# Per-layer gate of a decoder trunk: seven half-size products for each pair of full tiles, the 64-token tile last

## What is computed

```python
    h = h + moe
    u = rmsnorm(h, norm_ple)
    gate = jax.nn.sigmoid(jnp.einsum('bld,de->ble', u, w_ple_gate))   # 1024 x 1024
    h = h + gate * jnp.einsum('blp,pd->bld', p_l, w_ple_proj)         # 256 x 1024
    return h, ...
# then y = rmsnorm(h, norm_final)
```

## Time and profile before

| | us |
|---|---|
| median of 3 runs | 834.19 |
| lowest, highest | 830.54, 836.55 |
| the profiled execution | 832.21 |
| its span | 830.4 |

### The profile page before, as it was taken

The page is one execution under the profiler, slowest core; times in us unless marked ns, Lnnn a source line. Parts: engine busy times, 40 slices in busy tenths (PEclk is TensorE's granted clock), DMA queues, the critical chain, the costliest instruction groups (busy, mean ns, idle before and its releaser), DMA issues. The chain is left out here.

```text
span 830.4 us, 12851 instructions
## 1 busy us (share of the span) xinstructions
PE 810.4 (98%) x5194; PEld 509.7 (61%) x5194; DVE 385.0 (46%) x859; ACT 214.2 (26%) x463; POOL 151.0 (18%) x182
## 2 busy tenths in 40 slices
PE   9999999999999999999999999999999999998996
PEld 4545777887889987777777776456343333344452
DVE  3223457584666523664853558636341111106443
ACT  3211152339324311121101101122121111124554
POOL 0234321004055224200220043000100001004000
PEclk9999999999999999999999999999999999999999
DMA  9520354403020200522252024036899999987111
GB/s 359 206 101 9 124 181 152 134 39 109 2 103 3 84 20 13 202 80 94 101 203 87 16 101 176 9 127 252 307 367 399 425 420 415 410 313 221 57 39 51
DMA packets 20896, 135.23 MB, mean 163 GB/s; under 512 B 2420, under 2 KB 3060, under 8 KB 13668
## 3 DMA queue, kind: packets, MB, share of 16 engines
q1 hardware_dynamic: 13392, 103.34, 31.9%
q0 software_dynamic: 4720, 23.83, 8.0%
q10 hardware_dynamic: 2724, 7.21, 2.7%
HBM read 118.94 MB, written 19.63 MB: 167 GB/s over the span
## 5 line engine op out<-in xcount | busy, mean ns | idle before, releaser
L791 PE MATMUL pair<-mem 128*128 128x288 f32 x640 | 158.9, 408 | 0.0
L791 PEld LDWEIGHTS pair<-mem 128*128 128x128 f32 x640 | 120.5, 190 | 35.4 <-ACT mem L1435 2.1
L961 PE MATMUL single<-mem 128*128 128x288 f32 x448 | 110.1, 407 | 0.2
L961 PEld LDWEIGHTS single<-mem 128*128 128x128 f32 x448 | 84.8, 190 | 25.6 <-issue 1.6
L1346 PE MATMUL single<-mem 128*32 128x512 f32 x768 | 85.1, 594 | 0.9 <-DVE mem L2382 0.9
L1435 ACT ACTIVATE mem<-single 128x256 f32<-128x256 f32 (+5 forms) x109 | 44.6, 419 | 126.8 <-PE single L1209 48.5
L1435 ACT ACTIVATE mem<-pair 128x512 f32<-128x512 f32 (+5 forms) x78 | 33.5, 480 | 165.2 <-PE pair L791 63.1
L1414 PE MATMUL pair<-mem 128*128 128x512 f32 (+1 forms) x192 | 63.3, 524 | 0.0
L1346 PEld LDWEIGHTS single<-mem 128*32 128x32 f32 x768 | 23.7, 110 | 52.7 <-issue 51.6
L2375 DVE SCALAR_TENSOR_TENSOR mem<-single,mem 128x256 f32<-128x256 f32 x12 | 5.8, 484 | 102.3 <-PE single L1346 91.1
L1200 PE MATMUL pair<-mem 128*128 128x512 f32 x112 | 51.0, 601 | 0.0
(11 more groups left out here) (412 smaller groups left out, 1095.1 us busy)
## 6 DMA issues: line engine op xcount, KB each, us to landing
mem<-in_w_gu SPq DMA_DIRECT2D x17, 2048.0 KB, 14.4
mem<-in_w_down SPq DMA_DIRECT2D x17, 1024.0 KB, 14.0
y_slots<-mem SPq DMA_DIRECT2D x9, 512.0 KB, 11.2
y_slots<-in_zeros POOLq DMA_DIRECT2D x8, 512.0 KB, 8.5
mem<-in_w_ga SPq DMA_DIRECT2D x2, 2048.0 KB, 7.6
mem<-in_w_gb SPq DMA_DIRECT2D x2, 2048.0 KB, 7.8
mem<-in_w_wo SPq DMA_DIRECT2D x2, 2048.0 KB, 7.7
mem<-in_w_pg SPq DMA_DIRECT2D x2, 2048.0 KB, 18.2
```

The lines of the kernel that those rows point to most:

```text
L791: last = nc.tensor.matmul(pb[:, hf, 0:HALF], w(k), rhs[:, k, hf * HALF:(hf + 1) * HALF], start=(k == 0), stop=(k == kk - 1))
L961: last = nc.tensor.matmul(single[plan.buf[s]][:, 0:HALF], lhs[:, k, :], rhs[:, k, :], start=(k == 0 and j in (0, 1, 3, 4)), stop=(k == 3), ...
```

## The change

For a pair of full tiles (0 and 1, then 2 and 3) the gate product is taken as one product of a 2 x 2 block matrix (tile by half of the 1024 input channels) by a 2 x 2 block matrix (half of the input channels by half of the output channels). It is computed by seven half-size products (Winograd's form of Strassen's scheme) in place of eight. Each is 4 steps of 128x128 by 128x512. For that:

- DVE forms four sums of weights once (`pg_t1` to `pg_t4`, 128x2048 each, the third in two parts of 1024) and four sums of rows for each pair (128x512 each, one in place).
- Two of the seven accumulate onto a bank that already holds another product, and one more does after that. ACT copies the banks' states that are needed apart to `sgp` (`keep`, four for each pair), and DVE adds the bank to the kept part (`out`, four for each pair). The sigmoid then reads SBUF, not PSUM.
- The order of tiles is `LAST = [0, 1, 2, 3, 4]`: the 64-token tile is last, with its products as before.
- The squares and roots of the rows (`row_root`) are spread among the gates.
- `p_product(4)` stands ahead of `u3_transpose(0)`; tile 0's last combination is split in two halves, and its first four chunks are transposed after the first; the first product waits for the first four chunks alone.
- In the last expert phase the second of the two PSUM banks is copied by DVE rather than ACT, and the small transpose of the overflow block (`ov_hT`) moves from behind the last down product to its middle.
- The final stores are of 64 rows (tile 4) where they were of 128.

The core of the diff:

```diff
-LAST = [0, 1, 4, 2, 3]
+LAST = [0, 1, 2, 3, 4]
+PG_ORDER = ["p1", "p2", "p5", "u2", "p3", "p4", "p7"]
+KEPT = {(name, q): 6 + 4 * q + i for q in range(2) for i, name in enumerate(["p1", "p5", "u2", "p4"])}
...
+        pg_bank = [(pair[1][:, 0, :], pair[1][:, 1, :], pair[0][:, 0, :]), (pair[0][:, 1, :], pair[1][:, 1, :], pair[0][:, 0, :])]
...
@@ PE, last down product
+                    if p == NPH - 1 and n == 0:
+                        ov_hT(0)
...
             down(NPH - 1)
-            ov_hT(0)
             ov_down(0)
...
@@ PE, the stage
+            p_product(NT - 1)
             u3_transpose(0)
-            p_product(NT - 1)
...
+            def gate_part(bank, rows, weights, start):
+
+                for c in range(4):
+                    last = nc.tensor.matmul(bank, rows(c), weights(c), start=(start and c == 0), stop=(c == 3), skip_group_check=True)
+                return last
+
+            for q in range(2):
+                bank_a, bank_b, bank_c = pg_bank[q]
+                first, second = (lambda c: u3T[:, c, 2 * q * P:2 * q * P + P]), (lambda c: u3T[:, c, 2 * q * P + P:2 * q * P + 2 * P])
+                pe.wait_ge(sem("u3T"), 4 * q + 1)
+                pe.wait_ge(sem("w_pg"), 32)
+                pe.wait_ge(sem("pp"), 4 + q)
+                gate_part(bank_a, first, lambda c: w_pg[0][:, c, :], True).then_inc(sem("pg_mm"), 1)
+                u3_transpose(2 * q + 1)
+                pe.wait_ge(sem("u3T"), 4 * q + 2)
+                if q:
+                    pe.wait_ge(sem("pp"), KEPT["p4", 0])
+                gate_part(bank_b, lambda c: first(c + 4), lambda c: w_pg[0][:, c + 4, :], True).then_inc(sem("pg_mm"), 1)
+                pe.wait_ge(sem("pp"), 5)
+                pe.wait_ge(sem("pg_sum"), SUM_AT["s1", q])
+                gate_part(bank_c, lambda c: pg_s1[q][:, c, :], lambda c: pg_t1[:, c, :], True).then_inc(sem("pg_mm"), 1)
+                pe.wait_ge(sem("pp"), KEPT["p1", q])
+                pe.wait_ge(sem("pg_sum"), SUM_AT["s2", q])
+                gate_part(bank_a, lambda c: pg_s2[q][:, c, :], lambda c: pg_t2[:, c, :], False).then_inc(sem("pg_mm"), 1)
+                u3_transpose(2 * q + 2)
+                pe.wait_ge(sem("pp"), KEPT["p5", q])
+                pe.wait_ge(sem("pg_sum"), SUM_AT["s4", q])
+                gate_part(bank_c, lambda c: pg_s4[q][:, c, :], lambda c: w_pg[1][:, c + 4, :], False).then_inc(sem("pg_mm"), 1)
+                pe.wait_ge(sem("pg_sum"), max(SUM_AT["t4", 0], SUM_AT["c11", q]))
+                gate_part(bank_b, lambda c: second(c + 4), lambda c: pg_t4[:, c, :], True).then_inc(sem("pg_mm"), 1)
+                pe.wait_ge(sem("pp"), KEPT["u2", q])
+                pe.wait_ge(sem("pg_sum"), max(SUM_AT["t3", 0], SUM_AT["s3", q]))
+                gate_part(bank_a, second, lambda c: pg_t3[c // 2][:, c % 2, :], False).then_inc(sem("pg_mm"), 1)
...
@@ ACT: the helpers
-                copy(yb[b][:, 512:D], pair[b][:, 1, :]).then_inc(sem("y_ready"), 1)
+                if e_done < NPH:
+                    copy(yb[b][:, 512:D], pair[b][:, 1, :]).then_inc(sem("y_ready"), 1)
...
+            def keep(name, q):
+
+                act.wait_ge(sem("pg_mm"), 7 * q + PG_ORDER.index(name) + 1)
+                k, hf, bank = {"p1": (0, 0, 0), "u2": (0, 1, 0), "p4": (1, 0, 1), "p5": (1, 1, 2)}[name]
+                if q:
+                    act.wait_ge(sem("h4"), 2 * k + hf + 1)
+                copy(sgp[k][:, 512 * hf:512 * hf + 512], pg_bank[q][bank]).then_inc(sem("pp"), 1)
...
@@ DVE: the helpers
+            dve.wait_ge(sem("dn_mm"), NPH)
+            dve.wait_ge(sem("y_stored1"), 16 * ((NPH - 1) // 2))
+            V.tensor_copy(yb[1][:, 512:D], pair[1][:, 1, :]).then_inc(sem("y_ready"), 1)
...
+            def rows_1_2(q):
+
+                dve.wait_ge(sem("u3T"), 4 * q + 4)
+                V.tensor_tensor(pg_s1[q], rows(q, 1, 0), rows(q, 1, 1), ALU.add).then_inc(sem("pg_sum"), 1)
+                dve.wait_ge(sem("pg_sum"), SUM_AT["s1", q])
+                V.tensor_tensor(pg_s2[q], pg_s1[q], rows(q, 0, 0), ALU.subtract).then_inc(sem("pg_sum"), 1)
...
+            def out(name, q):
+
+                after, k, hf, kept, bank = {"c11": ("p2", 0, 0, "p1", 1), "c12": ("p3", 0, 1, "u2", 2),
+                                            "c21": ("p7", 1, 0, "p4", 0), "c22": ("p7", 1, 1, "p5", 0)}[name]
+                h = sgp[k][:, 512 * hf:512 * hf + 512]
+                dve.wait_ge(sem("pg_mm"), 7 * q + PG_ORDER.index(after) + 1)
+                dve.wait_ge(sem("pp"), KEPT[kept, q])
+                V.tensor_tensor(h, pg_bank[q][bank], h, ALU.add).then_inc(sem("pg_sum"), 1)
...
```

225 lines of the change are left out of this document (165 added, 60 removed).

## The result

| | us |
|---|---|
| before, median of 8 runs | 834.38 (830.54 to 836.55) |
| after, median of 8 runs | 837.85 (837.16 to 840.39) |
| ratio | 1.0062, 95% interval 1.0046 to 1.0078 |
| the profiled execution of after | 837.66, its span 835.8 |

The account below looks back on a forecast made before the run. PE bounds the kernel before; after the change ACT and DVE were to set the end from about 785. PE's 8.6 us are spent, the last copy comes 1.9 later, stores give 0.3: +1.6 on 834.19 makes 836, range 830 to 841.

Parts of the forecast that it names:

- in order of time: Last stage, engine by engine: PE ends 5.8 us earlier, but the last copy starts at 828.7 instead of 826.77, +1.9 us.
- four more loads and 20 us of sums in their line: ACT and DVE in the last stage: with these they end later than PE, spending 6 us of PE's saving and 1.6 more.
- so the first product starts at 755.5 instead of 757.08: 1.6 us: Start of the gate products: early input product and only four transposed chunks needed let them begin 1.6 us earlier.
- if the first product starts after 756: Sign at the first gate product, forecast for 755.5: a start later than 756 would show the prediction wrong.
- I take 0.2: End of the expert phase: copies side by side on ACT and DVE send the store earlier; gain 0.2 us, bounds 0 to 0.4.
- ahead of the transpositions it falls into the 3.01 us in which PE waits for the gather: The 64-token tile's input product (1.88 us), moved ahead of the first transposes, was to fit inside PE's 3.01 us wait.
- so there is 0.9 us to spare: cost nothing: DVE's first two weight sums end at 750.45, before the second gathered rows at 752.77, so they were to cost nothing.
- -0.3 for smaller stores: End of the kernel: the last stores are 128 KB, half of before, taking 0.3 us off the +1.9.
- PE keeps the end: Rival for the last stage: ACT and DVE stay hidden and PE sets the end, 825.9 to 831 us; chance 0.17.
- Late weights: Rival at the stage's start: w_pg landing after 746.7 delays the stage, 843 and more; 0.10, shared with dear hand-overs.
- A pause behind each table load: Rival on ACT: each function-table switch costs as much again as its load, 5.1 us more, 841; chance 0.02.
- The change does less than it says: Rival on PE's products: dismissed, since a half-size product is 4 of the same steps; no chance of its own given.

Follow-up runs that it names:

- experiments 1: The changed kernel with every root of the stage replaced by a square, so 14 table loads are gone: 832.85 us, ratio 0.9998 to the kernel before.
- experiment 2: The kernel before with its roots of the stage replaced by squares, ten of eleven table loads gone: 833.77 us against 834.26, ratio 0.9993.
- 3: The kernel also called fix: the changed kernel with four table loads fewer by order alone, two DVE scalings moved: 832.96 us.
- 12: The kernel also called tail: fix with ACT's and DVE's orders changed again and an own output buffer for the last tile: 829.5 us.
- experiment 5: The kernel before with only the changed kernel's tile order (64-token tile last) and its early input product: 834.82 us, ratio 1.0026.
- fix: The changed kernel with roots and DVE scalings reordered, four table loads fewer, same arithmetic: 832.96 us, ratio 0.9993 to the kernel before.
- tail: fix with ACT's and DVE's orders changed again, last tile's output buffer its own, PE's instructions unchanged: 829.5 us, ratio 0.9945 to the kernel before.
- experiment 6: The changed kernel with DVE's first two weight sums cut to slivers of 8 columns in 512: 837.3 us, ratio 1.0042 to the kernel before.
- experiment 8: fix with the later weight sums on POOL and half of the 64-token tile ahead of the last half-size product: 840.31 us, ratio 1.0083.

## Why the prediction came out as it did

**From the first product to the last copy, mechanism and size were right.** Against the working "in order of time", from the first product on:

| step | forecast | trace of after |
|---|---|---|
| PE waits for tile 2 | 1.2 | 1.16 |
| PE waits for tile 4 | 1.4 | 1.23 |
| DVE's sum of a bank and SBUF | 0.69 (0.60 to 0.77) | 0.684 |
| table loads | 15 | 15 |
| PE's last product behind the first's start | 61.9 | 61.9 |
| last copy behind PE's last product | 11.3 | 11.5 |
| first product to last copy | 73.2 | 73.4 |

What that stretch is made of was shown: the loads by experiments 1 and 2, the order by 3 and 12. The sum "four more loads and 20 us of sums in their line" named the right two causes; the third, the 64-token tile in last place (experiment 5: 2.2 us more from PE's last product to the last copy), was in the times of the prediction without being named as a cost. The change's saving on PE's side is real: in after, the products end at 820.48 (823.24 before) although they began 1.5 us later than before.

**The start of the stage was wrong.** The step is "so the first product starts at 755.5 instead of 757.08: 1.6 us"; it came at 758.57, 3.1 late, and "if the first product starts after 756" stood among the prediction's signs of being wrong (the other two, a chain of PE to the end and a wait for weight sums, did not come). The step that failed is PE's reserve ahead of the transposes. The reasons, by the rows of after and then of fix (DVE, then PE):

```profile
753.29 1.41 DVE L2536 SCALAR_TENSOR_TENSOR mem<-mem,wcomb 128x512 f32<-128x512 f32 x2 [1.12 <-DMA mem<-y_slots,posu]
```

```profile
740.74 12.45 PE L1401 MATMUL pair<-mem 128*128 128x512 f32 x40 [0.99 <-issue]
754.90 1.31 PE L1417 MATMUL single<-const,mem 128*128 128x128 f32 x8 [1.71 <-DVE mem L2536]
757.00 3.70 PE L1426 MATMUL pair<-mem 128*128 128x512 f32 x8 [0.78 <-DVE mem L2547]
```

- The forecast had tile 0 combined as a whole at 754.0. In after its first half was ready then (753.29 and half of the 1.41 of two instructions). The rows came 0.5 us later than in the trace of before (752.77): the store was issued at 739.58 instead of 739.44, so that the step "I take 0.2" of gain was a loss of 0.1, and the rows came 13.71 us after it instead of 13.33. The first four chunks could still be transposed at 754.0. But PE was not there: its input products ran until 756.76. The step "ahead of the transpositions it falls into the 3.01 us in which PE waits for the gather" had used up 1.88 of PE's 3.01 us in reserve, and then 2.3 us more of idle time at the branch (2.97 against 0.68) and 1.6 us at a low clock came on top: 1.9 + 2.3 + 1.6 - 3.0 = 2.8, measured 2.7. The other 0.4 us lie between the start of the transposes and the first product (1.87 us, of which PE waits 0.78 for DVE's evacuation), for which the sum had 1.5.
- Where PE was in time (fix, tail, both with the short idle time), the start is still only 757.00, since the gathered rows came 14.2 to 14.4 us after the store and not 13.33. The step "so there is 0.9 us to spare: cost nothing" looked at when DVE is free and not at what DVE's sums do to POOL's issue of the gathers beside them. Experiment 6 shows the slower issue, and its profile, without the first two sums, has the earliest start of the changed kernels, 756.01; that it is the slower issue which brings the rows late goes with the traces but is not shown by an edit.
- The idle time at the branch and the low clock behind it were no terms of the sum.

**The end term was wrong by half a microsecond.** "-0.3 for smaller stores": from the last copy to the end of the span it is 3.85 us in after (835.8 - 831.95) and 3.63 in before. Smaller stores gained nothing. So +3.1 at the start, +0.2 in the stretch, +0.5 at the end, on a forecast of +1.6: 832.21 + 5.4 = 837.6, and the profiled execution took 837.66.

**Part of the closeness is luck.** The forecast put a difference read from one profile, +1.6, onto the median of the kernel before. Between the profiles the difference is 5.4 us, 3.8 more than forecast. The median came out only 1.9 above the 836 because the profile of before is one without a low clock in the stage, while most of its executions (47 of those 68) have a lower mean clock and take some 2 us more.

**The rivals.** *PE keeps the end*: fallen; even without table loads after takes 832.85, and this rival had 825.9 to 831. *Late weights*: fallen; DVE began its first weight sum at 744.51 in after, so `w_pg` was there by then, earlier than the 745.8 I had worked out. Over the changed kernels the sums began between 744.02 and 746.86, and DVE always had time left before the rows came. Where late weights went with a late start, it was by POOL's issues beside the sums (experiment 6), which the rival did not name. *A pause behind each table load*: fallen; in after the square root at 807.07 follows its load (805.78, 1.28 long) by 0.01, and taking four loads out gave 4.25 us in the trace, less than their 5.1 and not twice it. The Trainium skill ("ScalarE: Activation LUTs", section What ACT_TABLE_LOAD costs) states 1380 ns of drain on each switch: the load agrees with the trace, the drain does not show in it. *The change does less than it says*: in its own arithmetic it does what it says.

**Why +0.6% in spite of 6.9 us saved on PE.** Of the stretch from the first product to the last copy, fix takes 4.25 us off and tail another 4.7, with the same products. The kernel with the seven-product form ends 0.55% faster than the one before, and the 3.7 us that after lost in this stretch were lost by where roots, sigmoids, sums and scalings stand in two engines' orders; the other 1.5 us between the profiles are the late start. Whether the kernel before would gain from orders tuned in the same way was not measured; that all its table loads gave nothing (experiment 2) speaks against much. Nor was the seven-product form run with a full tile in the last place. The single shares of tail's edits (the roots, the two moves on DVE, the buffer) are not separated either.

## What to carry to other kernels

When PE's work is cut and that of ACT and DVE grows, write out one line in order of time for each engine, with every wait, before any code: the shares of busy time (46% and 26%) gave no hint of a chain that took 11 us behind the last product. On such a chain look first for function-table switches that can be merged (two roots under one load, a dummy that loads while the engine waits anyway), then for calls that nobody waits for standing ahead of calls that somebody does. Ask what cover the last piece of work gives the other engines: here the smallest piece in the last place made the tail 2.2 us longer. And a reserve that a move eats up (3.0 us of PE's wait) has to be held against the spread of what comes ahead of it.

## What the runs showed of the hardware that I had not expected

**Idle time at a branch has two values.** Behind the overflow product PE comes to a branch around a loop that is not entered. In the 14 traces it then stood for 0.61 to 0.99 us in eight and for 2.75 to 2.97 us in six, with nothing to wait for. In all six a transfer of the instruction queue came some 2 us later than in the eight. The DMA queues of after between 740 and 741 us, then of fix between 738 and 739 (packets, MB, share of the engines):

```profile
q8 instruction: 1, 0.02, 6.8%
```

```profile
q8 instruction: 1, 0.02, 7.0%
```

The Trainium skill ("Runtime: NRT & Kernel Launch", section Instruction fetch mechanics) says that an engine's instructions are fetched in blocks of 16 KiB while the block before runs, and that a taken branch to what is not yet there has to wait for the fetch. The size of these packets, 0.02 MB, agrees with it; in after PE went on at 742.62, behind the packet, and in fix at 740.74. That PE waited for this very block is not shown. All four kernels that leave the end of the expert phase as it was before had the short value, and six of the ten that change it had the long one, among them both profiles of after; with the same stream of PE instructions both occur (after and fix). What decides it is open.

**The clock behind idle time.** By windows, after ran its first input products at the lower of TensorE's two levels, 1.2 GHz (a granted clock of 0.50), right behind the 2.97 us without work:

```profile
742.00:744.00 2.00, 1.38 (x3) 0.74 (x4) 0.00 (x0) 0.00 (x0) 0.00 (x0) 0.86 0.59 206
744.00:746.00 2.00, 2.00 (x3) 0.76 (x3) 1.49 (x1) 0.00 (x0) 0.00 (x0) 0.50 0.06 22
746.00:748.00 2.00, 2.00 (x5) 0.86 (x4) 1.97 (x2) 0.00 (x0) 1.12 (x2) 0.79 0.00 0
```

All six long idle times were followed by such a stretch; it cost 1.4 to 3.0 us in the input products. Four of the other eight had it at the first transposes or products instead, once behind no more than 1.08 and 0.78 us of idle time (experiment 6). The profile of the kernel before had none behind 3.01 us, but that of experiment 2, with the same PE instructions, had it behind 3.19: the transposes took 1.97 us instead of 1.09 and the input product 3.68 instead of 1.95.

```profile
756.00:758.00 2.00, 2.00 (x11) 1.07 (x11) 1.50 (x3) 0.00 (x0) 0.82 (x1) 0.50 0.82 270
```

A cost of some 2 us that comes and goes with PE's gaps belongs into a range.

**VectorE and GpSimd hold each other up.** In experiment 8 one DVE sum of two SBUF inputs took 9.25 us instead of 0.69 beside three sums on POOL, and experiment 6 shows the reverse, 2.01 instead of 0.93 us for the issue of a gather on POOL beside such a sum on DVE. The Trainium skill ("SBUF — State Buffer", section SBUF: two separate sides) says that the two engines share one pair of ports, which, where both read SBUF and the DVE instruction has two inputs there, one of them has to itself for a whole instruction. The trace of experiment 8 agrees, and goes further in that DVE did not get its turn between POOL's three sums. Work moved from the late DVE to the idle POOL was not hidden here, since both read SBUF.
